# Stage boundaries in finer steps: banks, halves and a two-step root in a transformer kernel on one core

## Chip, cores and metric

One core of a Trainium2 chip runs the whole kernel in one launch. The metric is the device time of one execution in microseconds. Lower is better.

## What is computed

Two blocks in sequence on x of 256 rows by 1024 columns in float32. The first block has two layers, each a token mixer (attention variants) and a SwiGLU feed-forward. The second has a feed-forward, a mixer (short convolution and a state-space scan) and a second feed-forward, and a final norm. Every stage has the same frame, and the frame is what the change touches:

```python
# first block, per stage (gate, scale, shift from c @ mod_w)
h = rms_norm(x, norm_w[layer, 0, 0]) * (1.0 + scale) + shift
y = mixer(h)                                   # or swiglu(h)
x = x + gate * rms_norm(y, norm_w[layer, 0, 1])
# second block
h = modulate(rms_norm_2(x, gain), sh, sc)
x = x + 0.5 * g[:, None, :] * swiglu_2(h, w_gate, w_up, w_down)   # mixer without the 0.5
...
return rms_norm_2(x, final_norm)

def rms_norm(x, w):
    y = x * rsqrt(mean(x * x, axis=-1) + 1e-6)
    return y * w
```

## The kernel before

**Stages.** In order: ab (attention), f0 (feed-forward), cd (attention), f1, then the second block's f2, in2 with glu and o2 (mixer), f3, end. Between them lie the boundaries; each has the name of the stage that follows it. A boundary takes the last products y out of PSUM banks 0 to 3, updates X, norms and modulates it, and turns it for the next stage.

**Numbers.** Products in float32 are made of three: each operand is split in a high part (HI, HH, HDH, rounded copies, cast by ScalarE) and a low part (LO, HLo, HDL, subtracted by VectorE). Weights come by the SyncE queue in 1 MB chunks into five raw buffers; each chunk has two halves of 1024 columns, and each half is cast (L957, HI) and subtracted (L1385, LO) into one of six slots. A raw buffer is loaded anew when the second half's LO is done, in the order of the plan. Chunks of the modulation matrix are used by VectorE alone, with a multiply-and-sum over the condition vector (gemv, L1375); the plan weaves them between the weights of f0, f1 and f2, from the front on.

**Layout.** X holds two row tiles of 128 rows, 1024 columns each. Row tile qt has its product y in banks 2qt and 2qt+1. TMP holds y times the gate row (gy).

**A boundary with its own norm** (add_normed: f0, cd, f1, f2). ScalarE squares each bank with a running sum (L1038 on), then Ln and Exp give a first 1/root. VectorE multiplies each bank by the gate row (gated_rows, L1485), adds the two sums (L1489), makes the mean (L1410), and refines the root with one Newton step of three small instructions (row_root, L1417, L1419, L1421), for each row tile; new_rows (L1494) then updates X. In f0 and f1 (`early`) X of tile 0 is updated before tile 1's products end. In cd and f2 both tiles are updated behind them. Boundaries in2, f3 and end have no norm of their own (add_gated: L1485, then one addition per tile, L1517).

**Then modulate.** PE turns X by 8 transposes per tile (L544), into the banks that y left. ScalarE squares X (row_sums), one Ln and one Exp serve both tiles (first_root(tag, 2)); VectorE refines both roots together and writes two diagonal tiles (dg, L1434); PE spreads them over the partitions with a product with -1 (rb), ScalarE copies that to RS. Then eight pieces follow: VectorE TMP (L1450), ScalarE HH, VectorE HLo (L1445), and the first products of the next stage run behind them. busy_wide(n) issues n products whose result is not used, between the steps; `fill` gives the three numbers. first_halves lists the first four weight halves of a stage; next_weights(tag, n) casts and subtracts the first n of them: three in the early add_normed, all four at the start of modulate, in front of the roots.

**Order.** Each engine's program is written out by hand in a function of its own (pe, act, dve, pool, sp) and runs in order. Each engine has one counting semaphore (P, A, D, G): `up` names the count behind an instruction, and waiting for a name means waiting until that engine has come so far in its own program.

## Time and profile before

| | |
|---|---|
| median of 3 runs | 1252.4 us (1251.65 to 1252.68) |
| profiled execution, span | 1253.3 us, 19977 instructions |
| TensorE matmul busy | 1159.8 us, 93% |
| TensorE weight load busy | 1050.5 us, 84% |
| VectorE busy | 932.8 us, 74% |
| ScalarE busy | 589.0 us, 47% |
| GpSimd busy | 74.6 us, 6% |
| DMA | 280.83 MB, mean 224 GB/s |

PE is busy nearly everywhere, but its busy time contains the unused products. A matmul's start is exact; its end is modelled. Helpers record all products on L408 and all ScalarE operations on L957, so those are told apart by their tiles and times. FB or SQ as a target of a square is only where the squared values are dropped.

### The profile page before, as it was taken

What the parts mean: (1) busy time and instruction counts of PE and PEld (TensorE: products, weight loads), DVE (VectorE), ACT (ScalarE), POOL (GpSimd) and SP (SyncE); (2) the same over time, 40 slices, a digit from 0 to 9 for tenths busy, and PEclk for the clock granted to TensorE, in tenths of its full rate; (3) what the DMA queues carried; (4) which work ended last, traced back from release to release, by engine and by line L of the source; (5) the groups of instructions that cost most, each with busy time, mean ns of one, the idle gap of its engine ahead of it and who ended that gap; (6) DMA issues with size and microseconds to landing.
All of it is one profiled execution on the core that took longest, in us unless ns stands there. A gap on an engine that the chain in (4) does not pass through costs nothing.

```text
span 1253.3 us, 19977 instructions
## 1 busy us (share of the span) xinstructions
PE 1159.8 (93%) x8358; PEld 1050.5 (84%) x8358; DVE 932.8 (74%) x1630; ACT 589.0 (47%) x968; POOL 74.6 (6%) x106
## 2 busy tenths in 40 slices
PE   2798888999998998899999989999989989999996
PEld 1677568899897996799999979999979967999996
DVE  5967868888786976788978688886765867765445
ACT  1534665344355457544444564444443355444433
POOL 0000000000000000097000000000000000000000
PEclk8799899999999999999999999999999998999998
DMA  9991434788884771467889537789722552765730
GB/s 375 360 371 51 172 135 159 306 310 320 273 333 163 298 263 45 151 249 288 307 229 361 212 139 299 301 246 334 275 103 102 110 177 89 267 240 196 185 133 34
DMA packets 40810, 280.83 MB, mean 224 GB/s; under 512 B 4736, under 2 KB 5264, under 8 KB 7952
## 3 DMA queue, kind: packets, MB, share of 16 engines
q1 hardware_dynamic: 37296, 269.27, 59.3%
q0 software_dynamic: 2416, 7.92, 2.1%
q10 hardware_dynamic: 1008, 2.37, 0.6%
q8 instruction: 65, 1.06, 0.3%
q14 instruction: 25, 0.20, 0.1%
HBM read 277.91 MB, written 1.10 MB: 223 GB/s over the span
## 4 chain that ended last, share of the span: by engine, by line
PE 71%; DVE 17%; ACT 5%; DMA 5%; issue 1%; SPq 0%; DVEq 0%; ACTq 0%
PE PS L408 70%; DVE LO L1385 5%; DMA raw<-WS 4%; DVE raw L1375 4%; ACT HI L957 2%; DMA SC<-scratch 1%; DVE TMP L1485 1%; DVE TMP L1450 1%; DVE HLo L1445 1%; DVE SC L1589 1%; PE PS L612 1%; ACT SC L957 1%; ACT SQ L957 1%; ACT HH L957 1%; ACT RS L957 0%
## 5 line engine op out<-in xcount | busy, mean ns | idle before, releaser
L408 PE MATMUL PS<-HH,HI 128*128 128x256 f32 x1748 | 502.4, 287 | 26.1 <-ACT HH L957 22.3
L408 PE MATMUL PS<-HLo,HI 128*128 128x256 f32 x1748 | 503.3, 288 | 0.4 <-DVE HLo L1445 0.3
L408 PE MATMUL PS<-HH,LO 128*128 128x256 f32 x1748 | 499.5, 286 | 0.2 <-issue 0.2
L1385 DVE TENSOR_TENSOR LO<-raw,HI 128x1024 fp32r<-128x1024 f32 x340 | 403.9, 1226 | 110.5 <-ACT HI L957 110.5
L957 ACT ACTIVATE HI<-raw 128x1024 fp32r<-128x1024 f32 x340 | 339.7, 1048 | 89.3 <-PE PS L408 57.0
L408 PEld LDWEIGHTS PS<-HH,HI 128*128 128x128 f32 x1748 | 340.3, 195 | 35.5 <-DVE LO L1385 19.6
L408 PEld LDWEIGHTS PS<-HH,LO 128*128 128x128 f32 x1748 | 340.4, 195 | 3.4 <-issue 0.5
L408 PEld LDWEIGHTS PS<-HLo,HI 128*128 128x128 f32 x1748 | 339.6, 194 | 3.6 <-DVE HLo L1445 2.2
L1375 DVE CUSTOM_DVE_ANT_0 raw<-raw,CB,SM 128x1024 f32<-128x1024 f32 x168 | 210.4, 1284 | 23.3 <-DMA raw<-WS 23.3
L408 PE MATMUL PS<-HI,HDH 128*128 128x512 f32 x352 | 140.2, 398 | 0.0
L408 PE MATMUL PS<-HI,HDL 128*128 128x512 f32 x352 | 139.5, 396 | 0.0
L408 PE MATMUL PS<-LO,HDH 128*128 128x512 f32 x352 | 138.9, 394 | 0.0
L957 ACT ACTIVATE HDH<-FB 128x256 fp32r<-128x256 f32 x88 | 36.8, 418 | 211.9 <-DVE FB L1546 211.9
L957 ACT ACTIVATE FB<-PS 128x256 f32<-128x256 f32 (+1 forms) x94 | 37.9, 403 | 126.7 <-PE PS L408 126.6
L408 PEld LDWEIGHTS PS<-HI,HDL 128*128 128x128 f32 x352 | 66.4, 189 | 15.9
L408 PEld LDWEIGHTS PS<-LO,HDH 128*128 128x128 f32 x352 | 66.5, 189 | 12.8
L408 PEld LDWEIGHTS PS<-HI,HDH 128*128 128x128 f32 x352 | 66.4, 189 | 12.4
L957 ACT ACTIVATE SC<-PS 128x512 f32<-128x512 f32 (+3 forms) x65 | 36.1, 571 | 84.1 <-PE PS L408 65.3
L1546 DVE TENSOR_TENSOR FB<-FB,PS 128x256 f32<-128x256 f32 x88 | 36.6, 416 | 51.9 <-ACT FB L957 51.8
L1549 DVE TENSOR_TENSOR HDL<-FB,HDH 128x256 fp32r<-128x256 f32 x88 | 37.6, 427 | 45.9 <-ACT HDH L957 45.9
L408 PE MATMUL PS<-HI,HH 128*128 128x512 f32 (+2 forms) x176 | 61.9, 352 | 7.0 <-DVE HLo L1467 5.8
L408 PE MATMUL PS<-LO,HH 128*128 128x512 f32 (+2 forms) x176 | 61.2, 348 | 0.0
(235 smaller groups left out, 1023.6 us busy)
## 6 DMA issues: line engine op xcount, KB each, us to landing
raw<-WS SPq DMA_DIRECT2D x255, 1024.0 KB, 5.4
SC<-scratch POOLq DMA_DIRECT2D x2, 1024.0 KB, 13.3
FB<-gates_out POOLq DMA_DIRECT2D x3, 512.0 KB, 4.9
SQ<-gates_out POOLq DMA_DIRECT2D x3, 512.0 KB, 9.9
X<-xT ACTq DMA_DIRECT2D x1, 1024.0 KB, 7.0
SC<-ssm POOLq DMA_DIRECT2D x2, 512.0 KB, 4.3
out<-TMP SPq DMA_DIRECT2D x2, 512.0 KB, 2.6
CB<-vecs SPq DMA_DIRECT2D x1, 512.0 KB, 6.6
```

Of the source, the lines that this page charges most:

```text
L408: return e.matmul(o, l, r, start=start, stop=stop, skip_group_check=True)
L612: x = e.transpose(ps[:, n * 128:(n + 1) * 128], s[:, n * 128:(n + 1) * 128], C("ident"))
L957: return e.activation(o, a, f, **k)
L1375: e.tensor_tensor_reduce(x, x, CB[:, :], 1.0, S("mb")[:, c:c + 1], O.mult, O.add, MV[:, c:c + 1]) \
L1385: e.tensor_tensor(LO[:, s % HL, :], raw_half(j, h), HI[:, s % HL, :].bitcast(fp32), O.subtract).then_inc(*D.up(("lo", s)))
L1445: e.scalar_tensor_tensor(HLo[:, k, :], TMP[:, k, :], MV[:, sh + k:sh + k + 1], HH[:, k, :].bitcast(fp32), O.add, O.subtract).then_inc(*D.u ...
L1450: e.scalar_tensor_tensor(TMP[:, k, :], turned(k), AV[:, k:k + 1], RS[:, 3, :], O.mult, O.mult) \
L1485: e.tensor_tensor(gy[qt][:, c], PS[:, b, :], grow(tag)[:, c], O.mult).then_inc(*D.up(("gy", tag, b)))
L1546: e.tensor_tensor(HF[:, j % 2, :], SIL[:, j % 2, :], bank((key, 0))[:, 256:512], O.mult) \
L1549: e.tensor_tensor(HDL[:, j % 3, :], HF[:, j % 2, :], HDH[:, j % 3, :].bitcast(fp32), O.subtract) \
L1589: e.tensor_tensor_reduce(s3[:, n, :], bank(("s", tag, i))[:, n * kw:(n + 1) * kw], BI[:, bh + h0 + n, bo:bo + kw], 1.0, sk[:, n:n + 1] if ...
```

## The change

- The last products (dn 10 of the feed-forwards, k = 6 and 7 of the last row tile in the output projections) go bank by bank: both weights for bank 2, then both for bank 3.
- Every update of X, and the final scaling and its write, is done in two halves of 512 columns; so are the squares of X. Each tile has its own Ln, Exp, Newton step, diagonal, product rb (128 columns) and copy (spread).
- The mean is no step of its own: the squares are scaled by 1/32, v0 is the first half's sum plus 1e-6, given to Ln as its bias beside the second half's sum; v = v0 plus that sum serves the Newton step.
- The Newton step has two instructions and gives -2 times the root; the gate row's factor -0.5, the diagonal's 0.5 and one more multiplication at the end make up for it.
- In add_normed of cd and f2, bank 3 is gated behind the update of tile 0.
- PE turns the two halves of a tile behind one wait each. The fills are (5, 6, 2) for (8, 4, 4) and (4, 2, 2) for (4, 0, 4), the last of them between the two rb products.
- The fourth weight half is cast and subtracted behind the eighth piece of modulate, not in front of the roots.

```diff
             w.wait_ge(*XIN.at("in"))
             w.wait_ge(*CONST.at("in"))
         else:
-            w.wait_ge(*D.at(("x", tag, qt)))
             w.wait_ge(*D.at(("gy", tag, 3)))
-            if tag not in ("in2", "f3"):
-                w.wait_ge(*A.at(("sq", tag, 2)))
         for k in range(8):
+            if tag != "ab" and k % 4 == 0:
+                w.wait_ge(*D.at(("x", tag, qt, k // 4)))
             e.transpose(turned(k)[:, qt * 128:qt * 128 + 128], X[:, qt, k * 128:k * 128 + 128], C("ident"))
-    busy_wide(fill[2])
-    ps = take(("rb", tag))
-    w.wait_ge(*D.at(("dg", tag)))
-    mm(ps[:, 0:256], nones[:, :], RS[:, 2, :], True, True).then_inc(*P.up(("rb", tag)))
-    banks.give(("rb", tag))
+    for qt in range(2):
+        if qt:
+            busy_wide(fill[2])
+        ps = take(("rb", tag, qt))
+        w.wait_ge(*D.at(("dg", tag, qt)))
+        mm(ps[:, 0:128], nones[:, :], dg[:, qt, :], True, True).then_inc(*P.up(("rb", tag, qt)))
+        banks.give(("rb", tag, qt))
 def ffn(tag, slow, gcol):
     def down(j):
...
     key = (tag, "dn", 10)
     wts = [weight(key, h) for h in range(2)]
     for qt in range(2):
-        for j in (20, 21):
-            w.wait_ge(*D.at(("hdl", tag, j)))
-            rows(tag, (HDH, HDL), j % 3, wts[j % 2], False, j == 21,
-                 [("down", tag, j), used(key, j % 2)] if qt else [], (qt,))
+        for h in range(2):
+            for j in (20, 21):
+                w.wait_ge(*D.at(("hdl", tag, j)))
+                rows(tag, (HDH, HDL), j % 3, wts[j % 2], False, j == 21,
+                     [("down", tag, j), used(key, j % 2)] if qt and h else [], (qt,), (h,))
 def scores(tag, U_, p):
...
 def out_half(name, ks, qt, gives=1, begins=0):
-    for k in ks:
-        key = (name, k // 2)
-        wt = weight(key, k % 2)
+    def half_ready(k):
+        wt = weight((name, k // 2), k % 2)
         w.wait_ge(*A.at(("hh", name, k)))
         w.wait_ge(*D.at(("hlo", name, 7 if qt or begins else max(k, 3))))
         if begins and not qt:
             w.wait_ge(*D.at(("hlo", name, 3)))
-        rows(name, (HH, HLo), k, wt, k == begins, k == 7, [used(key, k % 2)] if qt == gives else [],
+        return wt
+    ends = ks[-1] == 7 and qt == gives
+    for k in ks[:-2] if ends else ks:
+        wt = half_ready(k)
+        rows(name, (HH, HLo), k, wt, k == begins, k == 7, [used((name, k // 2), k % 2)] if qt == gives else [],
              (qt,))
+    if ends:
+        wts = [half_ready(k) for k in ks[-2:]]
+        for h in range(2):
+            for k, wt in zip(ks[-2:], wts):
+                rows(name, (HH, HLo), k, wt, k == begins, k == 7,
+                     [used((name, k // 2), k % 2)] if h else [], (qt,), (h,))
 walk.catch_up(walk.at_unit[3, 1])
 w.wait_ge(*SMALL.at("in"))
...
-modulate("f0", 32, (8, 4, 4))
+modulate("f0", 32, (5, 6, 2))
...
-modulate("f3", 152, (4, 0, 4))
+modulate("f3", 152, (4, 2, 2))
...
     w.wait_ge(*A.now())
     fn(r, z, F.Exp, scale=-0.5).then_inc(*A.up(("rexp", tag)))
-def row_sums(tag, qt, ready):
+def row_sums(tag, qt):
     w.wait_ge(*A.now())
-    w.wait_ge(*ready)
-    fn(junk(tag, qt), X[:, qt, :], F.Square, accum_out=s_[:, qt:qt + 1]).then_inc(*A.up(("s", tag, qt)))
-def first_root(tag, q):
-    c = cols[q]
+    for h in range(2):
+        c = slice(h * 512, h * 512 + 512)
+        w.wait_ge(*(XIN.at("in") if tag == "ab" else D.at(("x", tag, qt, h))))
+        fn(junk(tag, qt)[:, c], X[:, qt, c], F.Square, scale=1.0 / 32,
+           accum_out=x_[:, 2 * qt + h:2 * qt + h + 1]).then_inc(*A.up(("s", tag, qt, h)))
+def first_root(tag, qt, parts_):
     w.wait_ge(*A.now())
-    w.wait_ge(*G.at("consts"))
-    fn(z_[:, c], s_[:, c], F.Ln, bias=eps[:, 0:1], scale=1.0 / 1024).then_inc(*A.up())
+    w.wait_ge(*D.at(("v0", tag, qt)))
+    fn(z_[:, qt:qt + 1], parts_[:, 2 * qt + 1:2 * qt + 2], F.Ln, bias=v0_[:, qt:qt + 1]).then_inc(*A.up())
     w.wait_ge(*A.now())
-    fn(r_n[:, c], z_[:, c], F.Exp, scale=-0.5).then_inc(*A.up(("rexp", tag, q)))
+    fn(r_n[:, qt:qt + 1], z_[:, qt:qt + 1], F.Exp, scale=-0.5).then_inc(*A.up(("rexp", tag, qt)))
+def spread(tag, qt):
+    w.wait_ge(*P.at(("rb", tag, qt)))
+    fn(RS[:, 3, qt * 128:qt * 128 + 128], bank(("rb", tag, qt))[:, 0:128], F.Copy) \
+        .then_inc(*A.up(("free", ("rb", tag, qt))))
 def roots(tag):
     for qt in range(2):
-        row_sums(tag, qt, XIN.at("in") if tag == "ab" else D.at(("x", tag, qt)))
-    first_root(tag, 2)
-    w.wait_ge(*P.at(("rb", tag)))
-    fn(RS[:, 3, :], bank(("rb", tag))[:, 0:256], F.Copy).then_inc(*A.up(("free", ("rb", tag))))
+        row_sums(tag, qt)
+        first_root(tag, qt, x_)
+    for qt in range(2):
+        spread(tag, qt)
 def modulate(tag, sh, sc):
     high(walk.mods(sc + 8))
     if tag != "ab":
-        next_weights(tag, 4)
+        next_weights(tag, 3)
         roots(tag)
     for k in range(8):
         w.wait_ge(*D.at(("tmp", tag, k)))
         fn(HH[:, k, :], TMP[:, k, :], F.Identity, bias=MV[:, sh + k:sh + k + 1]) \
             .then_inc(*A.up(("hh", tag, k)))
+    if tag != "ab":
+        next_weights(tag, 4)
 def parts(tag, k, src, n=2):
     fn(HH[:, k:k + n, :], src, F.Copy).then_inc(*A.up(*[("hh", tag, k + i) for i in range(n)]))
...
     w.wait_ge(*A.now())
     for b in (2 * qt, 2 * qt + 1):
         w.wait_ge(*P.at(("acc", name, b)))
-        fn(junk(tag, qt)[:, b % 2 * 512:b % 2 * 512 + 512], PS[:, b, :], F.Square, accum_out=h_[:, b:b + 1]) \
-            .then_inc(*A.up(("sq", tag, b), ("s", tag + "y", qt)))
-    w.wait_ge(*D.at(("v", tag + "y", qt)))
-    first_root(tag + "y", qt)
+        fn(junk(tag, qt)[:, b % 2 * 512:b % 2 * 512 + 512], PS[:, b, :], F.Square, scale=1.0 / 32,
+           accum_out=h_[:, b:b + 1]).then_inc(*A.up(("sq", tag, b), ("s", tag + "y", qt, b % 2)))
+    first_root(tag + "y", qt, h_)
 def linear_out(name, ks, beyond=0):
     for i, k in enumerate(ks):
...
     w.wait_ge(*D.now())
     return r
-def mean(tag, q):
-    w.wait_ge(*A.at(("s", tag, min(q, 1))))
-    w.wait_ge(*D.now())
-    e.tensor_scalar(v_[:, cols[q]], s_[:, cols[q]], 1.0 / 1024, 1e-6, O.mult, O.add).then_inc(*D.up())
-def row_root(tag, q):
-    v, q_q, r = [x[:, cols[q]] for x in (v_, q_, r_n)]
-    w.wait_ge(*A.at(("rexp", tag, q)))
-    w.wait_ge(*D.now())
-    e.tensor_tensor(q_q, v, r, O.mult).then_inc(*D.up())
-    w.wait_ge(*D.now())
-    e.scalar_tensor_tensor(q_q, q_q, -0.5, r, O.mult, O.mult).then_inc(*D.up())
-    w.wait_ge(*D.now())
-    e.scalar_tensor_tensor(r, q_q, 1.5, r, O.add, O.mult).then_inc(*D.up())
+def mean(tag, qt, parts_):
+    a, b = [parts_[:, 2 * qt + h:2 * qt + h + 1] for h in range(2)]
+    w.wait_ge(*A.at(("s", tag, qt, 0)))
+    e.tensor_scalar(v0_[:, qt:qt + 1], a, 1e-6, None, O.add).then_inc(*D.up(("v0", tag, qt)))
+    w.wait_ge(*A.at(("s", tag, qt, 1)))
+    w.wait_ge(*D.now())
+    e.tensor_tensor(v_[:, qt:qt + 1], v0_[:, qt:qt + 1], b, O.add).then_inc(*D.up())
+def row_root(tag, qt):
+    v, q, r = [x[:, qt:qt + 1] for x in (v_, q_, r_n)]
+    w.wait_ge(*A.at(("rexp", tag, qt)))
+    w.wait_ge(*D.now())
+    e.tensor_scalar(q, v, r, r, O.mult, O.mult).then_inc(*D.up())
+    w.wait_ge(*D.now())
+    e.scalar_tensor_tensor(r, q, -3.0, r, O.add, O.mult).then_inc(*D.up())
     w.wait_ge(*D.now())
 def factors(sc, gain, ahead=2):
...
     e.scalar_tensor_tensor(AV[:, :], MV[:, sc:sc + 8], 1.0, gain, O.add, O.mult).then_inc(*D.up())
 def roots(tag):
-    mean(tag, 2)
-    row_root(tag, 2)
-    w.wait_ge(*CONST.at("in"))
     for qt in range(2):
-        e.tensor_scalar(dg[:, qt, :], C("ident"), r_n[:, qt:qt + 1], -1.0, O.mult, O.mult) \
-            .then_inc(*D.up(("dg", tag)))
+        mean(tag, qt, x_)
+        row_root(tag, qt)
+        w.wait_ge(*CONST.at("in"))
+        e.tensor_scalar(dg[:, qt, :], C("ident"), r_n[:, qt:qt + 1], 0.5, O.mult, O.mult) \
+            .then_inc(*D.up(("dg", tag, qt)))
 def modulate(tag, sh):
     if tag != "ab":
-        next_weights(tag, 4)
+        next_weights(tag, 3)
         roots(tag)
     w.wait_ge(*D.now())
...
                                HH[:, k, :].bitcast(fp32), O.add, O.subtract).then_inc(*D.up(("hlo", tag, k)))
     for k in range(8):
-        w.wait_ge(*A.at(("free", ("rb", tag))))
+        w.wait_ge(*A.at(("free", ("rb", tag, 1))))
         e.scalar_tensor_tensor(TMP[:, k, :], turned(k), AV[:, k:k + 1], RS[:, 3, :], O.mult, O.mult) \
             .then_inc(*D.up(("tmp", tag, k)))
         if tag == "ab" and k == 1:
...
         if k:
             rest(k - 1)
     rest(7)
+    if tag != "ab":
+        next_weights(tag, 4)
 def gate(tag, gcol, f, g):
     w.wait_ge(*D.now())
     if g is None:
...
+def gated_rows(tag, name, qt, normed, bs=None):
     w.wait_ge(*ROWIN.at(("grow", tag)))
-    for b in (2 * qt, 2 * qt + 1):
+    for b in bs or (2 * qt, 2 * qt + 1):
         w.wait_ge(*P.at(("acc", name, b)))
         if normed:
             w.wait_ge(*A.at(("sq", tag, b)))
         c = slice(b % 2 * 512, b % 2 * 512 + 512)
         e.tensor_tensor(gy[qt][:, c], PS[:, b, :], grow(tag)[:, c], O.mult).then_inc(*D.up(("gy", tag, b)))
-def own_norm(tag, qt):
-    w.wait_ge(*A.at(("s", tag + "y", qt)))
-    e.tensor_tensor(s_[:, cols[qt]], h_[:, 2 * qt:2 * qt + 1], h_[:, 2 * qt + 1:2 * qt + 2], O.add) \
-        .then_inc(*D.up(("v", tag + "y", qt)))
-    mean(tag + "y", qt)
 def new_rows(tag, qt):
-    e.scalar_tensor_tensor(X[:, qt, :], gy[qt], r_n[:, qt:qt + 1], X[:, qt, :], O.mult, O.add) \
-        .then_inc(*D.up(("x", tag, qt)))
+    for h in range(2):
+        c = slice(h * 512, h * 512 + 512)
+        e.scalar_tensor_tensor(X[:, qt, c], gy[qt][:, c], r_n[:, qt:qt + 1], X[:, qt, c], O.mult, O.add) \
+            .then_inc(*D.up(("x", tag, qt, h)))
 def add_normed(tag, name, sc, gain, early):
     factors(sc, gain)
     gated_rows(tag, name, 0, True)
-    own_norm(tag, 0)
-    row_root(tag + "y", 0)
+    mean(tag + "y", 0, h_)
     if early:
+        row_root(tag + "y", 0)
         new_rows(tag, 0)
         next_weights(tag, 3)
-    gated_rows(tag, name, 1, True)
-    own_norm(tag, 1)
+    gated_rows(tag, name, 1, True, (2,))
     if not early:
+        row_root(tag + "y", 0)
         new_rows(tag, 0)
+    gated_rows(tag, name, 1, True, (3,))
+    mean(tag + "y", 1, h_)
     row_root(tag + "y", 1)
     new_rows(tag, 1)
...
     for qt in range(2):
         gated_rows(tag, name, qt, False)
         w.wait_ge(*D.now())
-        e.tensor_tensor(X[:, qt, :], X[:, qt, :], gy[qt], O.add).then_inc(*D.up(("x", tag, qt)))
+        for h in range(2):
+            c = slice(h * 512, h * 512 + 512)
+            e.tensor_tensor(X[:, qt, c], X[:, qt, c], gy[qt][:, c], O.add).then_inc(*D.up(("x", tag, qt, h)))
         if tag == "f3" and qt == 0:
             next_weights(tag, 3)
...
 add_gated("end", "f3")
 w.wait_ge(*FIN.at("in"))
 for qt in range(2):
-    mean("end", qt)
+    mean("end", qt, x_)
     row_root("end", qt)
-    e.scalar_tensor_tensor(gy[qt], X[:, qt, :], r_n[:, qt:qt + 1], SC[:, 1024:2048], O.mult, O.mult) \
-        .then_inc(*D.up(("result", qt)))
+    e.tensor_scalar(r_n[:, qt:qt + 1], r_n[:, qt:qt + 1], -0.5, None, O.mult).then_inc(*D.up())
+    w.wait_ge(*D.now())
+    for h in range(2):
+        c = slice(h * 512, h * 512 + 512)
+        e.scalar_tensor_tensor(gy[qt][:, c], X[:, qt, c], r_n[:, qt:qt + 1], SC[:, 1024 + h * 512:1536 + h * 512],
+                               O.mult, O.mult).then_inc(*D.up(("result", qt, h)))
 def pool(e):
 w = Waits(e)
...
-gate("f0", 16, 1.0, S("nw")[:, 8:16])
+gate("f0", 16, -0.5, S("nw")[:, 8:16])
```

## Rows read from the trace of the kernel before

**Rows 1.** The page, part 4: shares of the chain that ended last, by engine.
```profile
PE 71%; DVE 17%; ACT 5%; DMA 5%; issue 1%; SPq 0%; DVEq 0%; ACTq 0%
```

**Rows 2.** Timeline, boundary cd, ScalarE, VectorE, PE: start us, us, engine, line, op [idle before].
```profile
394.55 0.60 ACT L957 ACTIVATE FB<-PS 128x512 f32<-128x512 f32 x1
...
395.37 1.29 DVE L1485 TENSOR_TENSOR TMP<-PS,SQ 128x512 f32<-128x512 f32 x2 [0.27 <-ACT FB L957]
...
396.76 0.29 ACT L957 ACTIVATE NR<-NR,eps 128x1 f32<-128x1 f32 x1 [0.94 <-DVE NR L1489]
...
396.83 1.27 DVE L1494 SCALAR_TENSOR_TENSOR X<-TMP,NR,X 128x1024 f32<-128x1024 f32 x1
...
398.79 1.29 DVE L1494 SCALAR_TENSOR_TENSOR X<-TMP,NR,X 128x1024 f32<-128x1024 f32 x1
...
399.99 1.22 DVE L1385 TENSOR_TENSOR LO<-raw,HI 128x1024 fp32r<-128x1024 f32 x1
...
401.36 0.30 ACT L957 ACTIVATE NR<-NR,eps 128x2 f32<-128x2 f32 x1
...
402.51 0.48 DVE L1434 TENSOR_SCALAR RS<-CN,NR 128x128 f32<-128x128 f32 x2
...
405.36 0.39 PE L408 MATMUL PS<-HH,HI 128*128 128x256 f32 x1 [1.61 <-ACT HH L957]
```

**Rows 3.** Waits of PE, 520 to 560 us, then 300 to 350: total, times, longest.
```profile
PE PS L408 <- DVE LO L1385: 0.2, 1, 0.2
...
PE PS L408 <- DVE LO L1385: 2.0, 2, 1.2
```

**Rows 4.** Timeline, boundary end: one gated bank.
```profile
1243.74 0.69 DVE L1485 TENSOR_TENSOR TMP<-PS,SQ 128x512 f32<-128x512 f32 x1
```

**Rows 5.** Timeline, boundary f0, fourth half's cast, X of tile 1, logarithm.
```profile
193.36 1.04 ACT L957 ACTIVATE HI<-raw 128x1024 fp32r<-128x1024 f32 x1
...
194.07 1.29 DVE L1494 SCALAR_TENSOR_TENSOR X<-TMP,NR,X 128x1024 f32<-128x1024 f32 x1
...
196.80 0.30 ACT L957 ACTIVATE NR<-NR,eps 128x2 f32<-128x2 f32 x1
```

**Rows 6.** Timeline, f0, eighth piece of modulate and first gemv.
```profile
205.64 0.51 ACT L957 ACTIVATE HH<-TMP,MV 128x256 fp32r<-128x256 f32 x1 [0.28 <-DVE TMP L1450]
...
206.59 1.28 DVE L1375 CUSTOM_DVE_ANT_0 raw<-raw,CB,SM 128x1024 f32<-128x1024 f32 x1
```

**Rows 7.** The chain in order of time: start us, us, what; f0, then f1.
```profile
206.67 1.20 DVE raw L1375
...
323.97 14.77 DMA raw<-WS
...
345.90 47.30 PE PS L408 x318
...
547.89 23.17 PE PS L408 x168
```

**Rows 8.** Timeline, first products of f1 and f2, and LO in f2.
```profile
525.69 0.45 PE L408 MATMUL PS<-HH,HI 128*128 128x256 f32 x1 [1.61 <-ACT HH L957]
...
730.52 0.48 PE L408 MATMUL PS<-HH,HI 128*128 128x256 f32 x1 [1.61 <-ACT HH L957]
...
750.02 3.49 DVE L1385 TENSOR_TENSOR LO<-raw,HI 128x1024 fp32r<-128x1024 f32 x3
```

**Rows 9.** The page, part 6: DMA issues: xcount, KB each, us to landing.
```profile
raw<-WS SPq DMA_DIRECT2D x255, 1024.0 KB, 5.4
...
out<-TMP SPq DMA_DIRECT2D x2, 512.0 KB, 2.6
```

**Rows 10.** Timeline, boundary end, the two final scalings.
```profile
1246.67 1.28 DVE L1984 SCALAR_TENSOR_TENSOR TMP<-X,NR,SC 128x1024 f32<-128x1024 f32 x1
...
1248.91 1.28 DVE L1984 SCALAR_TENSOR_TENSOR TMP<-X,NR,SC 128x1024 f32<-128x1024 f32 x1
```

**Rows 11.** Windows, f2: us, busy (x instructions) by engine, granted clock, DMA.
```profile
731.00:734.00 3.00, 3.00 (x16) 2.96 (x15) 3.00 (x8) 1.74 (x4) 0.00 (x0) 0.50 0.02 5
```

43 lines of the change are left out of this document (22 added, 21 removed).

## Prediction

> **What bounds the kernel now.** I read the chain that ended last first: the matrix products carry 71% of the span, VectorE 17% [rows 1]. Six times between stages, and once at the end, PE has no real product to run, so there the time is set by a relay between ScalarE and VectorE. I then read each boundary in order of time. The cd boundary [rows 2] shows the relay: bank 2 is squared from 394.55 us on, banks 2 and 3 are gated from 395.37, one root for rows 128 to 255 starts at 396.76, X of the first row tile is updated at 396.83 and X of the second at 398.79 to 400.08, its square fills the time to 401.36, where one logarithm for both tiles starts, the two diagonals at 402.51, and the first product of the next stage at 405.36. The weight subtraction for the fourth weight half lies at 399.99, where VectorE would wait for that square anyway. The reader is to see that the two engines take turns here, so an operation counts if the other engine waits for it, however short it is. Last I read who PE waits for just behind the boundaries: for LO, 0.2 us in f1 and 2.0 us late in f0 [rows 3], and what released the product after each such wait.
>
> **The change part by part.** Each term is the shift of the next stage's first real product.
>
> *A. Until X is new.* A VectorE half (512 columns) takes 0.69 us [rows 4], two back to back 1.29, a whole X update 1.28 [rows 2]: two halves of an update are about 1.41, 0.13 more than the whole, estimated. In cd and f2 (add_normed, not early) the new order is gate bank 2, root of tile 0, X0 in halves, gate bank 3, mean, root of tile 1, X1. Before, the logarithm and exponential of tile 1 ran on ScalarE while VectorE updated X0 (396.76 beside 396.83): free. Now bank 3 is gated only behind X0, the sum it feeds comes behind that, and Ln and Exp (0.30 and 0.20, with a hop each 0.6) stand bare between the mean and row_root. From 395.37: gate 0.6, root 0.4, X0 1.35, gate 0.6, sum 0.2, Ln and Exp 0.6, root 0.4: X1 starts at 399.4 instead of 398.79, and ends 0.13 later yet: +0.8. Bank 2 being complete earlier buys nothing, because ScalarE reaches its square only at 394.55, held by the exponential of tile 0, which waited for VectorE. In f0 and f1 (early), the new code has no X0 there; only one Newton instruction goes (-0.2) and halves add 0.13: -0.1. In in2 and f3 there is no root; halves add 0.1.
>
> *B. From X new to the logarithm of tile 1.* Before: 400.08 to 401.36, 1.28 us in cd [rows 2]; 195.36 to 196.80, 1.44 in f0, where the cast of the fourth half at 193.36 had pushed the squares back [rows 5]. After: ScalarE executes roots in program order: squares of X0, Ln of tile 0, Exp, then squares of X1. That Ln waits for v0 of tile 0, and VectorE issues v0 only behind the whole of add_normed or add_gated, so behind both halves of X1. The halves of X1's square therefore don't run beside the halves of its update; both are queued behind Ln. Sum: v0 0.2, Ln and Exp 0.55, two half squares 1.3 (0.60 each at 394.55 [rows 2] and some 0.05 for the accumulator), 2.05 us in all. That is +0.8 in cd, f2, in2 and f3, and +0.6 in f0 and f1.
>
> *C. From that logarithm to the first product.* Before 401.36 to 405.36, 4.0 us. One Newton instruction fewer -0.2; one diagonal instead of two behind the root -0.24 (0.48 for two, 402.51); the ones product and the copy over 128 instead of 256 columns: the trace has no such size, I take -0.2 and -0.1 (bounds 0 and -0.5 together: both are parts of the 2.4 us between the diagonals' end and 405.36). The two fill products between the tiles (0.5) are hidden: the first diagonal is 1.9 us ahead of the second. Sum -0.75.
>
> So cd and f2 +0.8 each, f0 and f1 -0.25 each, in2 and f3 +0.1 each: **+1.3 us**.
>
> *D. The fourth weight half put off.* It leaves the gap, where it was free on VectorE, and goes behind the eighth piece of modulate. In f0, ScalarE ends that piece at 206.15 and VectorE starts the first condition product (gemv) at 206.59 [rows 6]. Now ScalarE first casts (1.04 [rows 5]), VectorE waits for it until about 207.25, subtracts (1.22 [rows 2]), and the gemv starts at 208.4: **1.8 us later**. Everything VectorE has queued is behind it. What this costs PE depends on how far VectorE leads there. In f0 the chain holds no product of PE from that gemv (206.67 in it) to the one at 345.90 [rows 7]: VectorE and ScalarE carry it to the raw load issued at 323.97, which landed 14.77 us later behind loads that VectorE's own subtractions had released. I take the whole 1.8. In f1 PE waited 0.2 for LO at 547.89, the last link of VectorE's unbroken work since its modulate: 1.8 too. In f2 nothing waited: f1's first product, at 525.69, stands 22.0 us before PE was ready for that LO (547.7); f2's stood at 730.52, so PE was ready at 752.5, and the like LO was done at 751.2 (750.02 plus 1.2) [rows 8]. 1.3 of the 1.8 are covered: +0.5. cd, in2 and f3 have no condition product at the front and use the fourth half only some 9 us in: 0. Sum **+4.1**; bounds 0 (VectorE has slack that the chain hides) and 5.4 (f2 covers nothing). The put-off also holds SP's queue: the raw load that waits for this half goes out when its LO ends, in f0 at 208.4 instead of 196.5 (X1 at 194.07, 1.29, and 1.22 behind it), and every load behind it waits too. Landing takes 5.4 us in the middle [rows 9], and the products of that load come some 22 us behind the first one, so I price it at 0, up to +1.5.
>
> *E. The end.* Ln and Exp of each tile now stand behind VectorE's v0 (for tile 1 behind the first result), and one multiplication by -0.5 is added per tile. From the old 1246.67 and 1248.91 [rows 10]: the first result starts 0.35 later, the second 0.8, its end 0.9. The last write carries 256 KB: 512 KB took 2.6 us to landing and 1024 KB 5.4 [rows 9], which makes half a write worth up to 1.3; with a fixed part I take -0.6. Sum **+0.3**.
>
> *F. Nothing.* The last products bank by bank are the same 12 matmuls for each row tile; slots of the last two halves are released 0.7 us later at most, which nobody waits for. The folded factor -0.5 replaces one instruction by one. In the first stage v0 adds about 2 us to VectorE's relay at 23 us, but loads were landing later than VectorE could use them: 0, up to +0.4.
>
> Splitting is also what the Trainium skill warns of: VectorE: DVE Perf Modes, section The TRN2 errata, has instructions with SBUF sources pay a fixed latency each, (N+151)/0.96 ns for a float32 add, so halves cost 0.16 us each pair. The single half at 0.69 us agrees; but back to back a second half adds only 0.60 [rows 2, 4]. By the page the seven pairs on the path would cost 1.1 us, by the rows 0.8.
>
> **Sum.** 1.3 + 4.1 + 0.3 = 5.7 us. The profiled span of 1253.3 becomes 1259.0; the median of 1252.4 us lies 0.9 below the span, so I say **1258.1**. A measurement tells about 0.2% (2.5 us) from no change.
>
> **Rivals.**
> *Put-off is covered* (D is 0): VectorE's chain has slack in f0 and f1 that a single chain doesn't show, since an engine that is not busy all the time can catch up. For it: PE waits for LO in f0 only 2.0 us between 300 and 350 [rows 3]. Against: f1's wait of 0.2 sits at the end of unbroken work. Time: 1254.0, within 0.2%.
> *The clock, on the other side.* After every boundary TensorE runs at 1.2 GHz for a while (granted clock 0.50 from 731 to 734 us in f2 [rows 11]), behind the thin stretch before the first products. Those 3 us at half clock lose 1.5 us of products. The fills are spread anew (5, 6, 2 instead of 8, 4, 4). If that keeps the clock at 2.4 GHz at all six places, 9 us come back: 1249.1, faster. It takes all six to decide. Against: there are fewer fills, not more, and cd's and f2's gap grows. The Trainium skill, TensorE: Matmul & The Clock Gate, Part 1, says throttled is the default state and activity lifts it, which speaks for a fall wherever the rows are thinner.
> *Worse:* SP's late raw load delays f0, or a further half-clock stretch appears: 1258.1 plus 1.5 to 3.5, say 1261.
> *It does what it says:* v0 not being late would take B from the sum, four times 0.8 and twice 0.6: 5.7 - 4.4 = 1.3, 1253.7. The program order excludes it.
>
> **Chances.** Forecast (1255 to 1260) 0.66, covered 0.14, clock 0.04, worse 0.14, last 0.02. Slower by over 0.2% is the forecast and worse, 0.80; within 0.2% (covered, and the last) 0.16; faster 0.04. The range leaves out the clock case and the far end of worse: 1253.8 to 1261.5.
>
> **What would show it.** In cd and f2: VectorE gates bank 3 behind X0; X1 ends 0.8 later relative to the last product; last to first product 11.6 instead of 10.8, in f0 and f1 9.3 instead of 9.5. On ScalarE both squares of X1 start behind an Ln that VectorE's v0 released. In f0 and f1 the first gemv starts 2.2 us behind the eighth HH piece instead of 0.4, and PE's waits for LO grow by nearly 2 us in each. If PE waits for LO no longer than before, D is wrong; if the squares of X1 start before its second half is written, B is.

## The result, and the profile after

The changed kernel took 1264.3 us (median of 4 runs, 1262.4 to 1266.9), the kernel before 1252.1 us (median of 4, 1251.7 to 1252.7): a ratio of 1.0093, 95% interval 1.0077 to 1.0109. The change made the kernel slower by some 12 us. Forecast were 1258.1 us and a loss of 5.7.

All of the following goes by two lengths, read off TensorE's timeline in every kernel. A *gap* runs from the end of the last real product of a stage to the start of the first of the next, a *stage* from there to the end of its last real product; behind the last product of f3 comes the *tail*. The profiled execution took 1266.9 us, the longest of the four, with a span of 1265.1 (before: 1253.3). The difference of 11.9 us lies here:

| us | f0 | cd | f1 | f2 | in2 | f3 | tail | sum |
|---|---|---|---|---|---|---|---|---|
| gap before | 9.50 | 10.78 | 9.50 | 10.78 | 8.27 | 7.27 | 9.56 | 65.6 |
| gap after | 9.89 | 12.18 | 9.65 | 12.18 | 8.62 | 7.55 | 10.75 | 70.8 |
| stage before | 193.78 | 110.83 | 194.06 | 191.67 | 115.77 | 190.20 | | 996.3 |
| stage after | 194.66 | 111.96 | 197.13 | 192.92 | 116.34 | 190.19 | | 1003.2 |

So gaps and tail hold 5.2 us, the stages 6.9, and the first stage, ab, gave 0.2 back. These are the gap and stage lengths of one execution of each kernel. The gap at cd, first on VectorE (an L1508 row gates a bank, L1513 updates X, L1429 is the half mean, L1439 and L1441 are the Newton step, L1454 the diagonal); it answers to [rows 2]:

```profile
396.46 0.69 DVE L1508 TENSOR_TENSOR TMP<-PS,SQ 128x512 f32<-128x512 f32 x1 [1.25 <-ACT FB L968]
397.19 0.27 DVE L1439 TENSOR_SCALAR NR<-NR 128x1 f32<-128x1 f32 x1
397.49 0.16 DVE L1441 SCALAR_TENSOR_TENSOR NR<-NR 128x1 f32<-128x1 f32 x1
397.69 1.41 DVE L1513 SCALAR_TENSOR_TENSOR X<-TMP,NR,X 128x512 f32<-128x512 f32 x2
399.02 0.68 DVE L1508 TENSOR_TENSOR TMP<-PS,SQ 128x512 f32<-128x512 f32 x1
399.62 0.14 DVE L1429 TENSOR_SCALAR NR<-NR 128x1 f32<-128x1 f32 x1
400.42 0.27 DVE L1439 TENSOR_SCALAR NR<-NR 128x1 f32<-128x1 f32 x1 [0.47 <-ACT NR L968]
400.92 1.41 DVE L1513 SCALAR_TENSOR_TENSOR X<-TMP,NR,X 128x512 f32<-128x512 f32 x2
402.25 0.15 DVE L1429 TENSOR_SCALAR NR<-NR 128x1 f32<-128x1 f32 x1
...
405.49 0.28 DVE L1454 TENSOR_SCALAR RS<-CN,NR 128x128 f32<-128x128 f32 x1
```

and then on ScalarE (the FB<-X rows are the squares of X of the second tile) and TensorE:

```profile
399.86 0.53 ACT L968 ACTIVATE NR<-NR 128x1 f32<-128x1 f32 x2 [2.92 <-DVE NR L1429]
...
402.50 0.53 ACT L968 ACTIVATE NR<-NR 128x1 f32<-128x1 f32 x2 [0.74 <-DVE NR L1429]
403.06 0.63 ACT L968 ACTIVATE FB<-X 128x512 f32<-128x512 f32 x1
...
403.69 0.62 ACT L968 ACTIVATE FB<-X 128x512 f32<-128x512 f32 x1
...
404.43 0.53 ACT L968 ACTIVATE NR<-NR 128x1 f32<-128x1 f32 x2
...
407.83 0.39 PE L407 MATMUL PS<-HH,HI 128*128 128x256 f32 x1 [1.51 <-ACT HH L968]
```

The orders that the prediction derived from the code are there. Bank 3 is gated behind X0 (399.02), and the logarithm and exponential of the second tile stand bare in front of the root (399.86, with VectorE idle for 0.47 until 400.42). Both squares of X1 start behind the logarithm and exponential of the first tile at 402.50, for which ScalarE had waited 0.74 us until the half mean at 402.25. That half mean comes behind both halves of X1.

The front of f0 on VectorE, answering to [rows 6]; L1394 is the first condition product:

```profile
207.31 1.22 DVE L1404 TENSOR_TENSOR LO<-raw,HI 128x1024 fp32r<-128x1024 f32 x1 [0.46 <-ACT HI L968]
208.46 1.28 DVE L1394 CUSTOM_DVE_ANT_0 raw<-raw,CB,SM 128x1024 f32<-128x1024 f32 x1
```

The condition product starts 7.47 us behind the stage's first product at 200.99, where it started 5.79 behind it before (206.59 and the first product at 200.80). Some 24 us into f1 TensorE runs dry. The first fence is TensorE's timeline there, answering to [rows 3], the second the granted clock in the stretch behind it (the columns are the busy times of PE, PEld, DVE, ACT and POOL, PEclk, the DMA share and GB/s), and the third the stretch around the same place before the change, where TensorE waited only 0.24 us, at 547.89:

```profile
551.14 0.40 PE L407 MATMUL PS<-HI,HDL 128*128 128x512 f32 x1
553.28 0.39 PE L407 MATMUL PS<-HH,HI 128*128 128x256 f32 x1 [1.75 <-DVE LO L1404]
```

```profile
553.28:556.70 3.42, 3.42 (x18) 3.42 (x19) 3.32 (x4) 0.28 (x2) 3.11 (x5) 0.58 0.86 352
```

```profile
547.00:550.40 3.40, 3.16 (x24) 2.70 (x23) 3.37 (x4) 1.09 (x2) 3.15 (x4) 1.00 0.73 263
```

TensorE waits 1.75 us for a LO, and works through the next 3.42 us at a granted clock of 0.58, where it had 1.00 before. That stretch costs, as an estimate, another 3.42 x 0.42 = 1.4 us of products, which the prediction's sum doesn't hold.

The same happens 42 us into f0, where TensorE waits 2.15 us for a LO until 242.67 (0.80 us at the same place before, at 240.81):

```profile
242.00:245.50 3.50, 2.83 (x15) 2.83 (x16) 3.40 (x6) 0.00 (x0) 0.00 (x0) 0.67 0.99 403
245.50:249.00 3.50, 3.50 (x27) 3.50 (x27) 2.46 (x6) 2.32 (x3) 0.00 (x0) 0.84 0.86 337
```

In between lie 3.4 us, from 243.21 to 246.62, at a granted clock of 0.50.

### The profile page after: what moved, and what is told of

Its sections match the earlier page's. It is cut to its first block, busy times and chain, and to the rows that moved or that the text cites. A ratio compares the mean times of both kernels' runs of the same rounds, so it can differ in the third digit from the quotient of the medians.

```text
span 1265.1 us, 20088 instructions
## 1 busy us (share of the span) xinstructions
PE 1165.7 (92%) x8360; PEld 1056.4 (83%) x8360; DVE 940.4 (74%) x1668; ACT 597.1 (47%) x1021; POOL 72.7 (6%) x106
## 3 DMA queue, kind: packets, MB, share of 16 engines
q8 instruction: 65, 1.06, 0.3%
## 4 chain that ended last, share of the span: by engine, by line
PE 76%; DVE 15%; ACT 5%; DMA 2%; issue 1%; SPq 0%; DVEq 0%; ACTq 0%
PE PS L407 75%; DVE LO L1404 3%; DVE raw L1394 3%; DMA raw<-WS 1%; DVE TMP L1470 1%; DMA SC<-scratch 1%; DVE SC L1612 1%; ACT HI L968 1%; DVE HLo L1465 1%; ACT NR L968 1%; DVE TMP L1508 1%; DVE SC L1597 1%; ACT HH L968 1%; DVE X L1513 1%; ACT SQ L968 1%
## 5 line engine op out<-in xcount | busy, mean ns | idle before, releaser
L1394 DVE CUSTOM_DVE_ANT_0 raw<-raw,CB,SM 128x1024 f32<-128x1024 f32 x168 | 210.1, 1283 | 17.9 <-DMA raw<-WS 17.8
L407 PEld LDWEIGHTS PS<-LO,HDH 128*128 128x128 f32 x352 | 66.5, 189 | 12.9
```

What stands on the lines that cost most here:

```text
L407: return e.matmul(o, l, r, start=start, stop=stop, skip_group_check=True)
L1394: e.tensor_tensor_reduce(x, x, CB[:, :], 1.0, S("mb")[:, c:c + 1], O.mult, O.add, MV[:, c:c + 1]) \
```

## The experiments

All ratios below are against the kernel before, in runs on the same chip. The sum of gaps and tail was read off each kernel's own profile:

| kernel | put-off | gaps and tail, against 65.6 | ratio (95%) | in us |
|---|---|---|---|---|
| change | yes | +5.2 | 1.0093 (1.0077 to 1.0109) | +11.6 |
| before, put-off alone | yes | -0.4 | 1.0059 (1.0042 to 1.0077) | +7.4 |
| change, three instructions in a root | yes | +6.2 | one run, 1264.0 us | |
| change, both banks gated first | yes | +4.2 | 1.0101 (1.0082 to 1.0120) | +12.6 |
| change, squares first | yes | +2.7 | 1.0077 (1.0058 to 1.0097) | +9.6 |
| change, weight back | no | +12.5 | 1.0112 (1.0092 to 1.0132) | +14.0 |
| change, weight behind the means | no | +12.9 | 1.0124 (1.0104 to 1.0143) | +15.5 |
| before, new fills | no | +0.5 | 1.0001 (0.9988 to 1.0014) | +0.1 |
| rearranged, first | no | -0.6 | 0.9991 (0.9978 to 1.0004) | -1.1 |
| rearranged, second | no | -2.9 | 0.9972 (0.9958 to 0.9985) | -3.5 |
| the same, fills of the change | no | -1.5 | 0.9982 (0.9969 to 0.9996) | -2.3 |

The last column is the ratio less 1, times 1252. Where the weight is not put off, the time follows the gaps within 3 us; where it is, 6 to 8.5 us come on top. Both halves of that are taken up in turn. A single profile is a rough measure of the whole: the first stage, ab, ended between 187.7 and 194.7 us in these twelve profiles, and two kernels that differ in fills alone lie 3.6 apart there (191.1 and 194.7). So whole times are compared by the ratios, and profiles by single gaps and stages.

**The put-off alone on the kernel before.**

```
-                    next_weights(tag, 4)
+                    next_weights(tag, 3)
                     roots(tag)
...
                 rest(7)
+                if tag != "ab":
+                    next_weights(tag, 4)
```

> The kernel before, with the put-off of the fourth weight half alone. Theory: 4 to 6.5 us slower than before, about 1257.5, with PE waiting for LO 1.5 to 2.1 us early in f0, in f1 and in f2. Rival (the put-off costs something only on top of boundaries that have become longer): within 1 us of before.

Measured: 1.0059, +7.4 us (5.3 to 9.6). The put-off costs time by itself, and the middle of the interval lies above the upper end of 6.5. Of the waits, f1's was as expected (1.75 us), f0's longer (2.42, ending at 240.34, 42 us into the stage) and f2's only 0.54. Its stages were 194.41 (f0), 197.14 (f1) and 192.92 us (f2); three kernels with changed boundaries and the put-off have 194.4 to 194.7, 197.12 to 197.14 and 192.92 to 192.93, and the fourth, the three-step kernel below, 194.39, 196.24 and 192.92. Seven kernels without it (the kernel before among them) have 192.0 to 193.8, 194.0 to 194.5 and 191.0 to 192.8. Mean against mean, and without the three-step kernel in f1 (with it 2.8), the put-off costs 1.5 us in f0, 3.0 in f1 and 1.2 in f2, 5.7 in all.

In f0 the cost is not in the waits: before the change TensorE waited for LO three times there (0.80, 0.74 and 1.22 us, 2.8 in all), with the put-off once, for 1.9 to 2.4 us. But all five kernels with the put-off have 3.4 us at a granted clock of 0.50 right behind that wait (from 241.25 here, from 243.21 in the changed kernel), and none of the seven without it has such a stretch between the front and the end of f0. TensorE's wait in f1:

```profile
547.53 0.39 PE L408 MATMUL PS<-HH,HI 128*128 128x256 f32 x1 [1.75 <-DVE LO L1387]
```

That is 23.85 us behind the first product of its stage (523.68); in the changed kernel it is 23.84 (553.28 less 529.44), before 22.20 (547.89 less 525.69). The place is set by VectorE's queue, 1.64 us later with the put-off, whether the boundary is the old or the new one (only the three-step kernel has 24.28). In f2 the same: 22.7 us behind the first product in all five kernels with the put-off.

**The change with the weight put back.**

```
-                    next_weights(tag, 3)
+                    next_weights(tag, 4)
                     roots(tag)
...
                 rest(7)
-                if tag != "ab":
-                    next_weights(tag, 4)
```

> The changed kernel, but the fourth weight half is cast and subtracted in the gap again, as before the change. Theory (the put-off holds VectorE's queue 1.8 us at the front of f0, f1 and f2, and PE's waits for LO draw a half-clock stretch behind them): 5 to 7 us less than the changed kernel, so about 1258; f0's stage falls from 194.7 to about 193.8 us, f1's from 197.1 to about 194.1, f2's from 192.9 to about 191.7, and the half-clock stretches that start at 243.2 and 553.8 us are gone; the gaps between the stages stay within 0.3 us of the changed kernel's. Rival (the relay at the boundaries and the clock behind them make the whole difference, the put-off is hidden): less than 2 us.

Measured: 1.0112, no faster than the change. Half of the expectation came true. f1's stage fell from 197.13 to 194.37 us, f0's to 192.02, the waits for LO in f1 and f2 were gone (f0 kept two, of 0.93 and 0.52 us), as were the half-clock stretches behind them, and the stages together became 9.2 us shorter. Of that, 5.5 us lie in f0, f1 and f2, and 2.7 in cd, where no wait for LO had been. f2's stage stayed at 192.81 and didn't fall to 191.7: the half-clock stretch at its front was 6.8 us long (0.50 from 734.70 to 741.50, with the first product at 735.38), where the changed kernel begins f2 at 1.00 and the kernel before has 3.4 us of it. But the gaps and the tail became 7.4 us longer, 1.1 to 1.4 at each of the six boundaries. The expectation that they would stay within 0.3 us was wrong. VectorE and then ScalarE in the gap at f0:

```profile
195.00 1.22 DVE L1402 TENSOR_TENSOR LO<-raw,HI 128x1024 fp32r<-128x1024 f32 x1
196.14 0.14 DVE L1427 TENSOR_SCALAR NR<-NR 128x1 f32<-128x1 f32 x1
```

```profile
196.38 0.53 ACT L968 ACTIVATE NR<-NR 128x1 f32<-128x1 f32 x2 [0.92 <-DVE NR L1427]
196.94 0.63 ACT L968 ACTIVATE SQ<-X 128x512 f32<-128x512 f32 x1
```

The subtraction now stands ahead of the half mean, and the half mean is what ScalarE's next logarithm waits for (0.92 us idle at 196.38). Before the change that logarithm waited for nothing of VectorE's, and the subtraction ran beside the square of X1, between the rows of [rows 5] at 194.07 and 196.80:

```profile
195.28 1.22 DVE L1385 TENSOR_TENSOR LO<-raw,HI 128x1024 fp32r<-128x1024 f32 x1
```

So the new mean took away the cover under which the subtraction was free. With the new mean the fourth half costs about as much in the gap as put off; with the old mean, it is free in the gap and costs 7 us put off.

**The weight behind the means.** The squares of both tiles first (below), the cast in the gap again, and

```
                 for qt in range(2):
                     mean(tag, qt, x_)
+                if tag != "ab":
+                    next_weights(tag, 4)
                 for qt in range(2):
                     row_root(tag, qt)
```

> The changed kernel with both squares first (as in the run a_squares_first), the fourth weight half cast in the gap again, and VectorE's subtraction of it placed behind the means of both row tiles instead of ahead of them. Theory (undoing the put-off alone brought nothing because the subtraction of 1.22 us then stood ahead of the mean for which ScalarE's logarithm waits, and each gap grew by 1.1 to 1.4 us): the gaps are those of a_squares_first plus 0.2 to 0.6 us each, the stages those of the kernel before in f1 (194.1), so about 4 us less than a_squares_first, 1256. Rival (the fourth half in the gap costs as much as it saves wherever it stands): 1260 or more, each gap over 1 us longer than in a_squares_first.

Measured: 1.0124, each gap 0.8 to 2.5 us longer than in the run with the squares alone; the rival's side. f0's gap grew from 9.27 to 11.75. VectorE and TensorE there:

```profile
195.92 0.16 DVE L1431 TENSOR_TENSOR NR<-NR 128x1 f32<-128x1 f32 x1 [0.46 <-ACT SQ L968]
196.00 1.22 DVE L1403 TENSOR_TENSOR LO<-raw,HI 128x1024 fp32r<-128x1024 f32 x1
197.32 0.27 DVE L1438 TENSOR_SCALAR NR<-NR 128x1 f32<-128x1 f32 x1
```

```profile
198.17 0.80 PE L407 MATMUL PS<-RS,nones 128*128 128x128 f32 x2 [3.24 <-DVE RS L1456]
198.62 1.20 PE L407 MATMUL PS<-HH 128*128 128x512 f32 x2
199.62 0.63 PE L407 MATMUL PS<-RS,nones 128*128 128x128 f32 x2
```

Behind the last mean everything of both tiles is still to be done: two roots, two diagonals, and on TensorE two ones products with two fills between them, which at half clock took 1.0 us (198.62 to 199.62). The subtraction is no cheaper there. It needs a place with nothing of the relay behind it.

**Squares of both tiles first** (ScalarE squares both before the first logarithm, VectorE makes both means before the first root):

```
                 for qt in range(2):
                     row_sums(tag, qt)
+                for qt in range(2):
                     first_root(tag, qt, x_)
```

> The changed kernel, but in roots ScalarE squares both row tiles before the logarithm of the first, and VectorE adds up both means before the first root. Theory (the square of the second tile's first half then runs beside the update of its second half, and is queued behind no logarithm): each of the six gaps 0.6 us shorter, 3.5 to 4 us in all, about 1260.5. Rival (the square of the second tile is bound by the update of its second half, and the later root of the first tile takes the gain back): less than 1 us.

Measured: gaps shorter by 0.62 (f0), 0.38 (cd, f1, f2) and 0.33 (in2, f3), 2.4 in all, and 1.0077 (its interval overlaps that of the changed kernel, so the finding rests on the gaps). That lies between the two forecasts: the logarithm in front of the squares costs, as the theory says, but a part goes to the first tile's root, which is now later. In cd VectorE begins that root 1.37 us behind the end of X1 (399.39), where in the changed kernel it began 0.73 behind it (403.06), and the second tile's root queues behind it and its diagonal (400.29).

**Both banks gated first in cd and f2:**

```
-                gated_rows(tag, name, 1, True, (2,))
+                gated_rows(tag, name, 1, True)
+                mean(tag + "y", 1, h_)
                 if not early:
                     row_root(tag + "y", 0)
                     new_rows(tag, 0)
-                gated_rows(tag, name, 1, True, (3,))
-                mean(tag + "y", 1, h_)
```

> The changed kernel, but in cd and f2 VectorE gates both banks of the second row tile and adds up its mean before it updates X of the first, the order of before. Theory (Ln and Exp of the second tile stand bare between mean and root in the changed order): the gaps at cd and f2 fall from 12.2 to about 11.5 us each, the whole time by 1.5 us, other gaps unchanged. Rival (the place of the second bank costs nothing, ScalarE is late anyway): 0.

Measured: the gaps of cd and f2 fell from 12.18 to 11.82, by 0.36 each, half of what the theory said; the whole can't be told from the changed kernel.

**Three instructions in a root again:**

```
-                e.tensor_scalar(q, v, r, r, O.mult, O.mult)
+                e.tensor_tensor(q, v, r, O.mult)
+                w.wait_ge(*D.now())
+                e.scalar_tensor_tensor(q, q, 1.0, r, O.mult, O.mult)
```

> The changed kernel with three instructions in each root of a row tile again, none of them with two pointers to scalars. By the prediction's sheet an instruction fewer in a root is worth 0.2 us: cd and f2 would be 0.6 us longer (three roots on the relay), f0 and f1 0.4. By the rows of the changed kernel (the instruction with two pointers lasts 0.27 where others last 0.16) it is worth 0.08: cd and f2 0.25 longer, f0 and f1 0.15.

Measured, in a single profiled run: cd and f2 0.24 longer, f0 and f1 0.11 and 0.14, as by the rows and not as by the sheet. The instruction saved is worth 0.08 us, because the one that stays, with two pointers to scalars, lasts 0.27 (397.19 above) where its neighbour lasts 0.16.

This kernel also separates the wait from the clock. Its LO came 24.28 us into f1 (551.24 less 526.96), but no half-clock stretch followed, and from there its stage took 196.24 - 24.28 = 171.96 us. In the changed kernel it took 197.13 - 23.84 = 173.29, before 194.06 - 22.20 = 171.86. So the half-clock stretch costs 1.3 to 1.4 us in f1, beside the 1.6 of the wait.

**The new fill products alone on the kernel before:**

```
-            modulate("f0", 32, (8, 4, 4))
+            modulate("f0", 32, (5, 6, 2))
...
-            modulate("in2", 128, (4, 0, 4))
+            modulate("in2", 128, (4, 2, 2))
```

> The kernel before with the fill products of the change alone (5, 6, 2 for 8, 4, 4; 4, 2, 2 for 4, 0, 4). Forecast of the prediction's steps: nothing, within 1 us. Rival (the fills set the half-clock stretches behind the boundaries, and these make part of the loss in cd and in2): 2 us or more slower, with longer half-clock stretches at the boundaries.

Measured: 1.0001. The gaps of cd and f2 grew by 0.25, the rest didn't move. The fills make no measurable part of the loss, and the clock at the boundaries is not kept up by them either: each of the six has a stretch at 0.50 with either set of fills, 3.4 us in all at five and 6.8 at cd.

**Rearranged, first version.** Beside the two edits above: X of the first tile whole, its square summed in one piece so that ScalarE's logarithm needs nothing of VectorE's, and the end of the kernel as before. The core of it on VectorE:

```
             def roots(tag):
+                half_mean(tag, 1, x_)
                 for qt in range(2):
-                    mean(tag, qt, x_)
+                    full_mean(tag, qt, x_)
                     row_root(tag, qt)
...
                     roots(tag)
+                    next_weights(tag, 4)
```

> A version put together from the findings: both banks gated ahead of X of the first tile in cd and f2; X of the first tile whole, of the second by halves; the first tile's square and logarithm by ScalarE alone, without a mean from VectorE, in f0 and f1 ahead of the second tile's banks; the half mean of the second tile at once behind its update; the fourth weight half cast where ScalarE waits and subtracted behind the second diagonal, where VectorE waits for ScalarE's copy; the end with whole writes and the old root. Theory (every step taken off the relay between VectorE and ScalarE counts in full): gaps of f0 and f1 8.6, cd and f2 10.3, in2 7.6, f3 6.6, no LO stall behind the boundaries: 4 us faster than before, about 1247.5. Rival (what is taken from the relay comes back in half-clock stretches or LO waits): within 1.5 us of before.

Measured: 0.9991 (0.9978 to 1.0004), not to be told from before. f0, f1, in2 and f3 came within 0.2 us of the forecast (8.79, 8.79, 7.76, 6.75), the waits for LO in f1 and f2 were gone (f0 still had 1.88 us at 238.27 and 1.22 at 342.34), but cd and f2 were 11.55 and 11.66 instead of 10.3. TensorE at cd:

```profile
395.33 1.94 PE L542 MATMUL PS<-CN,X 128*128 128x128 f32 x8 [3.17 <-DVE X L1536]
396.92 2.35 PE L407 MATMUL PS<-HH 128*128 128x512 f32 x6
399.11 1.03 PE L542 MATMUL PS<-CN,X 128*128 128x128 f32 x8
```

Six fills between the turning of the first tile and of the second took 2.35 us at half clock, and the second turning, whose X was there at 397.2, started at 399.11. TensorE had become the last link of a relay in which, before, it had waited 0.89 us for VectorE's diagonals (at 403.05).

**Rearranged, second version** (best2; the first version is best1), with the fills 8, 2, 0 in cd and f2 and none between the ones products elsewhere, and the first tile's root ahead of the second's half mean:

```
                 for qt in range(2):
                     full_mean(tag, qt, x_)
                     row_root(tag, qt)
+                    if qt == 0:
+                        half_mean(tag, 1, x_)
```

> best1, but VectorE makes the mean and root of the first tile before the half mean of the second (in best1 it waited 0.6 us in cd for that square with nothing behind it begun), and TensorE's fill products are 8, 2, 0 in cd and f2 and none between the two ones products (in best1 the 6 fills at half clock ended at 399.1 us, 2.0 us after X of the second tile was there). Theory (in cd and f2 TensorE had become the last link): gaps of cd and f2 10.3 instead of 11.6, f0 and f1 8.5, in2 7.5, f3 6.5, the end 9.5; 4 us faster than before. Rival (fewer fills lengthen the half-clock stretches behind the boundaries and give it back): same time as best1, with gaps as above and stages 2 us longer.

> best2 with the fill products of the change (5, 6, 2 and 4, 2, 2), as in best1. Theory (fills are the last link in cd and f2 only): gaps of cd and f2 11.3, the others within 0.2 us of best2, the whole 2 to 2.5 us above best2. Rival (VectorE's order was the link in cd): cd and f2 within 0.3 us of best2.

Measured: 0.9972 (0.9958 to 0.9985), 3.5 us faster than before, and with the change's fills 0.9982. f0 and f1 have gaps of 8.60, in2 7.58, f3 6.58, the tail 9.46; cd and f2 10.97, with the change's fills 11.65. So in cd and f2 the fills are worth 0.7 us and the order by itself nothing (11.54 and 11.66 in the first version, which has the same fills); at the other four boundaries it is the other way round, 0.2 us by the order and nothing by the fills. The theory named the right link, but 10.3 was still too low. In whole time the two kernels can't be told apart (the intervals overlap), where 2 to 2.5 us were expected. Here is what is left of the theory in cd, on ScalarE:

```profile
398.46 0.29 ACT L968 ACTIVATE NR<-NR,eps 128x1 f32<-128x1 f32 x1
398.79 0.20 ACT L968 ACTIVATE NR<-NR 128x1 f32<-128x1 f32 x1
399.02 0.63 ACT L968 ACTIVATE FB<-X 128x512 f32<-128x512 f32 x1
```

ScalarE does the first tile's logarithm until 399.0, while the first half of the second tile, whose update began at 397.80, had been ready for half a microsecond.

## Why the prediction was wrong

The direction was right, and so was the account of which orders would change. The size was half of the truth: 5.7 us forecast, about 12 measured, outside the range. The step that failed most is D: it priced the put-off by TensorE's waits alone, +4.1, and the put-off alone measured +7.4 (5.3 to 9.6), with a half-clock stretch behind the wait in f0 and in f1 that the sum doesn't have. The rest are sizes in A, C and E, 3.6 us too small together. By its steps:

**A, until X is new.** Forecast for cd and f2 +0.6 until the update of X1 starts and 0.13 for the halves. Measured from the last product: 398.79 - 394.58 = 4.21 before, 400.92 - 395.65 = 5.27 after, +1.06, and +0.13 for the halves (two halves of X take 1.41 us, as the sheet has it, though its 0.69 for one half is a row that reads PSUM, and X lies in SBUF). The mechanism is as forecast, the term mis-sized. From the gating of bank 2 (396.46) to X1 (400.92) the sheet has 4.15 us; it took 4.46, each piece a little longer than its rounded entry. And the entries, added to 395.37, give 399.52, where the prediction wrote 399.4. Undoing the order of the banks gives 0.36 us of this back, not all. For f0 and f1 -0.1 was forecast and +0.1 came: X1 starts 2.74 us behind the last product instead of 2.76, so that the saving of 0.2 is missing, and the halves add their 0.13.

**B, from X new to the logarithm.** Forecast 2.05 us. Measured in cd 404.43 - 402.33 = 2.10; in f0 2.09. Right in mechanism and size, and the squares-first run shows the mechanism: the gaps fall when no logarithm stands ahead of those squares.

**C, from the logarithm to the first product.** Forecast -0.75. Measured -0.60 in cd (404.43 to 407.83, 3.40 us) and -0.34 in f0. The Newton instruction fewer was priced at 0.2 and is worth 0.08 (three-step run). In f0 the ones product of the second tile ran in the half-clock stretch:

```profile
198.74 0.74 PE L407 MATMUL PS<-RS,nones 128*128 128x128 f32 x2 [0.97 <-DVE RS L1454]
```

It lasted 0.74 us; the same product of cd, at 405.83, lasted 0.49. With A and B this makes gaps of +4.0 us instead of +1.3. In in2 and f3 they grew by 0.35 and 0.28 where 0.1 was forecast.

**D, the put-off.** The first condition product is late by 1.68 us in f0 (7.47 less 5.79) and by as much in f1, as the sheet's 1.8 says. Then the sum went wrong twice upwards. In f1 the wait drew a half-clock stretch behind it that cost 1.4 us: the sum stopped at the wait and priced no consequence of it, though the further half-clock stretch stood among the rivals. In f2 the cover of 1.3 us was smaller. The LO and TensorE's wait for it in the changed kernel (they answer to [rows 8]):

```profile
760.15 3.49 DVE L1404 TENSOR_TENSOR LO<-raw,HI 128x1024 fp32r<-128x1024 f32 x3
```

```profile
761.42 0.39 PE L407 MATMUL PS<-HH,HI 128*128 128x256 f32 x1 [1.64 <-DVE LO L1404]
```

The product at 761.42 starts when the first of those three subtractions is done. It stands 22.66 us behind the stage's first product; TensorE's last product ahead of it ended 21.0 us behind the first one (759.79 less 738.76), where before the change it came to this place after 21.8 (752.30 less 730.52). The clock goes with this: before, the stage's first 3 us ran at half clock [rows 11], now the half-clock stretch lies from 731.3 on, inside the longer gap, and the stage begins at full clock:

```profile
731.00:734.70 3.70, 3.70 (x16) 3.01 (x14) 2.71 (x9) 2.83 (x11) 0.00 (x0) 0.54 0.00 0
738.80:742.00 3.20, 3.18 (x23) 2.94 (x24) 3.20 (x9) 1.83 (x4) 0.00 (x0) 1.00 0.02 5
```

TensorE came 0.8 us earlier and only waited longer. The prediction took TensorE's arrival for a constant. On the old boundaries, where the half-clock stretch stays inside the stage, the put-off made TensorE wait 0.54 us, as the forecast of +0.5 says. In f0 the 1.8 was near in size (0.9 us in the profile of the change, 1.5 over all kernels) and wrong in mechanism. TensorE's waits for LO, which were to grow by nearly 2 us, fell from 2.8 to 2.15: the late ones of [rows 3] are gone, an early one that the prediction doesn't name grew from 0.80 to 2.15, and what costs time goes with the half-clock stretch behind it. That the size was near is luck. In all D was forecast as +4.1 and measured, alone, as +7.4 (5.3 to 9.6). The three stages account for 5.7 of that; the rest can't be put to a place.

**E, the end.** Forecast +0.3, measured +1.2. VectorE's first and second result, and the issues of the writes on SP's queue:

```profile
1257.84 1.41 DVE L2011 SCALAR_TENSOR_TENSOR TMP<-X,NR,SC 128x512 f32<-128x512 f32 x2
...
1260.67 1.41 DVE L2011 SCALAR_TENSOR_TENSOR TMP<-X,NR,SC 128x512 f32<-128x512 f32 x2
```

```profile
1258.62 3.82 SPq L2122 DMA_DIRECT2D out<-TMP  x4
```

```profile
out<-TMP SPq DMA_DIRECT2D x4, 256.0 KB, 2.5
```

From the last product (1254.37) they start 3.47 and 6.30 us later, where [rows 10] has 2.96 and 5.20 behind 1243.71: +0.51 and +1.10 for the forecast +0.35 and +0.8. The other term failed altogether. The half write was to save 0.6 us; 256 KB took 2.5 us to landing, 512 KB took 2.6 [rows 9]. From the end of the last scaling to the end of the span it is 3.04 us (1262.08 to 1265.12), before 3.07 (1250.19 to 1253.26). The 5.4 us of 1024 KB, from which the saving was derived, were loads in the middle of the kernel and not writes.

**F.** The fills are worth nothing measurable, as said. The last products bank by bank were not tried alone, nor was the first stage, where the profiles spread too widely to show 0.4 us.

**The rivals.** That the put-off is covered is refuted by its run alone. "Worse", with a further half-clock stretch, came true in f1, where the stretch cost 1.4, and a second one stands in f0. But it was taken as an alternative to the forecast and not as what follows from its own wait. Left out was any error that several small terms share: A, C and E each fell short on the same side, together 3.6 us.

What stays open is some 1 to 2 us of the stages, and why a wait draws a half-clock stretch in one place and not in another. cd's stage was 110.8 us before and 112.0 after, but 109.2 to 110.5 in all the others, and its half-clock stretches lie elsewhere in each; so that difference is no finding.

## What to carry to other kernels

An operation is free only as long as nobody waits for the one behind it on its engine: before a new wait is put into a relay, look at what stood ahead of its source for nothing, because that is no longer free (here the subtraction of 1.22 us, at six boundaries). A wait on a fully used TensorE can cost more than its length, since the clock can fall behind it (9 times of 15 here); price both, and take TensorE's arrival not as fixed. Of a relay between two engines, split and reorder the side that is late, and then look again at the third engine, whose filler work has become the last link.
